# First turns of a feed-forward stage regrouped, attention scores over 128 rows, mLSTM gate rows by transfer

## The chip, the cores and the metric
The kernel runs on one core of a Trainium2 chip. Its time is the device time of one launch in microseconds (us). Matmuls run on TensorE (PE in the rows), elementwise work on VectorE (DVE), activations and copies on ScalarE (ACT), and small work on GpSimd (POOL). SyncE (SP) issues the weight transfers, GpSimd the others.

## The reference, cut to what matters
Two blocks of two layers each, on 256 tokens (two tiles of 128) and width 1024. Twelve stages run one after the other: in each layer a feed-forward stage, a mixer and a feed-forward stage. All eight feed-forward stages have an inner width of 2816.

```python
def swiglu_2(h, w_in, w_out):
    g, u = jnp.split(h @ w_in, 2, axis=-1)
    return (jax.nn.silu(g) * u) @ w_out
```

Block one ends each stage with a LayerNorm over the residual. Block two scales by an RMS norm ahead of and behind each stage. The mixer of block two has eight attention heads of width 64, whose scores of query and key are masked and weighted over all 256 tokens, and four mLSTM heads of width 128 in two directions. For head h and direction d the kernel computes, over all pairs of tokens s and t at once and with a as the key's gate value and m the running maximum,

```
w[s, t] = exp(a[s] - m[t])  where s <= t (d = 0) or s >= t (d = 1), else 0
num[t]  = sum_s w[s, t] * (k[s] . q[t]) * [v[s], 1]
cell[t] = sum over both directions of num[t] / max(|its last column|, exp(m)-term)
```

The cells are normed per head, gated, joined to the attention's output and multiplied with the output weights.

## The kernel before
**Numbers.** Every matmul with weights is done in three passes, high part by high part, high by low and low by high, of float32r operands. ScalarE copies a weight unit (128x1024) from its staging buffer to its high part `w_hi` (L286), VectorE subtracts to get the remainder `w_lo` (L293). There are 4 staging buffers and a ring of 10 units. SyncE loads unit u once the remainder of unit u - 4 is made. All engines walk through their lists of instructions in an order that is written out by hand and wait for each other by semaphores; there is no planner. `hi_upto` and `lo_upto` say up to which unit the weights are to be split at this point of the list.

**Feed-forward stage** (`pe_ffn`, `act_ffn`, `dve_ffn`). The inner width goes in 11 steps of 256 columns, 0 to 10. A step has four units of gate-and-up weights and two of down weights. In the unit order v = 0 to 65, the down units of step i come behind the gate-and-up units of step i + 1. Tile 1 of the tokens runs six units behind tile 0 (in stage 0 both run together for the first ten units). A tile of `hidden`, which is silu(gate) times up for 128 tokens and 256 columns, written (tile, step), must be turned before its down products: by TensorE (two transposes, L444) or by VectorE (`dve_turn_blocks`, 16 transposes of 32 rows, L468, for one tile or for two tiles at once). Then ScalarE takes the high part (L546) and VectorE the remainder `mt_lo` (L550), and TensorE waits for the latter. `pe_turns` (L429) lists which tiles TensorE turns: (0,0), (0,10) and (1,10), in stage 0 also (1,0). `block_turns` (L447) gives VectorE's groups: the unit at which a group begins, its length in units, and its tiles. In the later stages (0,1) and (1,0) are one group that begins at unit 9 and lasts four units, in stage 0 (0,1) and (1,1) are one from unit 8 on. Behind that, (0,i+1) and (1,i) go together. The last one, (1,9), goes by itself from unit 62 to 64.

**Mixer of block two** (`pe_mix2`, `act_mix2`, `dve_mix2`, `pool_mix2`). TensorE makes queries and keys, turns them, and ScalarE copies the turned ones to `aqk_t` (L1594), two heads over each other in 128 rows. Then 32 slots follow, of convolution inputs and then of values and output gates; a head of attention is scored (`a_scores`, L1438, over its own 64 rows), turned (L1448) and multiplied with the values (L1459) between them. The last head is scored in slot 22. VectorE makes the mLSTM's gate rows by scans at the first head. Then for each mLSTM head `m_pair` does four score matmuls (two of two passes, L1512) and four (two of two passes, L1515) that spread the negated maxima of both directions over 128 rows; `args` on VectorE adds the key's column and the mask (L1860), ScalarE takes the exponential (L1685), `weights` multiplies with the scores (L1871), and `m_out` (L1533) forms the sums. Output units (`out_unit`) stand between the heads. `cells`, `forward`, `cells_sum`, `squares`, `cell_var` and `gated_cells` make the normed and gated cell, `turn_cells` (L1541) turns it: heads one and two together, then three, then four. GpSimd loads rows, sets margins and takes reciprocal roots.

## Time and profile before

| what | value |
|---|---|
| median of 3 runs | 2150.64 us (2150.47 to 2152.52) |
| profiled execution, its time | 2148.35 us |
| its span, first to last instruction | 2146.6 us |
| mean granted TensorE clock | 0.997 |
| TensorE busy | 2112.1 us, 98% of the span |
| VectorE, ScalarE, GpSimd busy | 1685.6, 1077.0 and 65.6 us (79%, 50%, 3%) |
| DMA | 393.70 MB, mean 183 GB/s |

A line of a view names engine, kernel line, operation and tiles as out<-in, with the shape and a count. Matmuls are pipelined: a matmul of 512 columns is shown 0.39 us long, while the next one starts 0.227 us after it. So costs on TensorE are read from start to start. A float32 matmul is two instructions in the trace. "Idle before" is the time in which the engine had nothing to do, and the name behind it is what ended it. The granted clock is 1.00 at 2.4 GHz and 0.50 at 1.2 GHz.

### The profile page before, as it was taken

Reading aid. Unit: us, or ns where it says so; the run is one execution under the profiler, and the core shown is the slowest. Engines: PE = TensorE matmul, PEld = TensorE weight load, DVE = VectorE, ACT = ScalarE, POOL = GpSimd, SP = SyncE. Lnnn points to the kernel's source line nnn. Section 1 sums busy time; section 2 is a strip of 40 time slices with the busy share of each in tenths; the row PEclk is TensorE's granted clock in tenths of the full one; section 3 lists DMA queues with packets and bytes.
Section 4 is the critical chain, followed back from the end, with each engine's and each line's share of the span. In section 5 each row is a group of like instructions: output and inputs, shape, how many; then the busy total and the mean of one; then the engine's idle time right before and its main releaser. Section 6 shows DMA issues by size and latency. Waiting matters only on the chain.

```text
span 2146.6 us, 28816 instructions
## 1 busy us (share of the span) xinstructions
PE 2112.1 (98%) x10580; PEld 1778.2 (83%) x10580; DVE 1685.6 (79%) x3108; ACT 1077.0 (50%) x1540; POOL 65.6 (3%) x107
## 2 busy tenths in 40 slices
PE   8999999999999999999999999999999999999998
PEld 6888999888788899988877888877887888888887
DVE  6888766888888867678888886788887888678886
ACT  5444553544544455454454446564445445665443
POOL 0000010000000001000000000010000000001000
PEclk9999999999999999999999999999999999999999
DMA  7766754666666574666656656337666665644663
GB/s 232 236 198 179 214 177 148 208 195 196 196 192 194 167 233 141 193 196 196 191 185 195 195 178 189 111 119 224 189 193 188 186 194 160 186 132 140 195 190 105
DMA packets 313951, 393.70 MB, mean 183 GB/s; under 512 B 17828, under 2 KB 272052, under 8 KB 313812
## 3 DMA queue, kind: packets, MB, share of 16 engines
q1 hardware_dynamic: 309120, 375.52, 57.6%
q0 software_dynamic: 4528, 16.29, 2.4%
q8 instruction: 84, 1.38, 0.2%
q14 instruction: 55, 0.45, 0.1%
q10 hardware_dynamic: 164, 0.06, 0.0%
HBM read 390.75 MB, written 1.05 MB: 183 GB/s over the span
## 4 chain that ended last, share of the span: by engine, by line
PE 84%; DVE 9%; DMA 3%; issue 2%; ACT 2%; SPq 0%; POOL 0%; DVEq 0%; POOLq 0%; ACTq 0%
PE bank L309 23%; PE bank L311 23%; PE bank L310 23%; DVE w_lo L293 5%; PE bank L303 3%; PE bank L304 3%; PE bank L305 3%; DVE hidden L468 2%; DMA stage<-in_ffn_w_in 1%; DMA stage<-in_w_in 1%; DMA stage<-in_ffn_w 1%; PE bank L1438 1%; ACT w_hi L286 1%; PE bank L1459 1%; PE bank L482 1%
## 5 line engine op out<-in xcount | busy, mean ns | idle before, releaser
L286 ACT ACTIVATE w_hi<-stage 128x1024 fp32r<-128x1024 f32 x711 | 746.2, 1058 | 681.8 <-PE bank L311 534.0
L293 DVE TENSOR_TENSOR w_lo<-stage,w_hi 128x1024 fp32r<-128x1024 f32 x711 | 865.4, 1224 | 259.1 <-ACT w_hi L286 252.6
L309 PE MATMUL bank<-w_hi,xt_hi 128*128 128x512 f32 x1760 | 691.8, 393 | 0.6 <-DVE w_lo L293 0.2
L311 PE MATMUL bank<-w_hi,xt_lo 128*128 128x512 f32 x1760 | 685.8, 390 | 0.0
L310 PE MATMUL bank<-w_lo,xt_hi 128*128 128x512 f32 x1760 | 685.6, 390 | 0.0
L468 DVE STREAM_TRANSPOSE hidden<-hidden 32x128 f32<-32x128 f32 (+1 forms) x1280 | 377.6, 295 | 21.0
L309 PEld LDWEIGHTS bank<-w_hi,xt_hi 128*128 128x128 f32 x1760 | 330.9, 188 | 71.7 <-issue 3.1
L311 PEld LDWEIGHTS bank<-w_hi,xt_lo 128*128 128x128 f32 x1760 | 330.6, 188 | 69.6
L310 PEld LDWEIGHTS bank<-w_lo,xt_hi 128*128 128x128 f32 x1760 | 331.0, 188 | 66.3
L309 PE MATMUL bank<-w_hi,mt_hi 128*128 128x512 f32 x768 | 305.6, 398 | 20.0 <-DVE mt_lo L550 20.0
L311 PE MATMUL bank<-w_hi,mt_lo 128*128 128x512 f32 x768 | 301.2, 392 | 0.0
L310 PE MATMUL bank<-w_lo,mt_hi 128*128 128x512 f32 x768 | 300.6, 391 | 0.0
L309 PEld LDWEIGHTS bank<-w_hi,mt_hi 128*128 128x128 f32 x768 | 145.1, 189 | 56.0 <-DVE w_lo L293 22.9
L311 PEld LDWEIGHTS bank<-w_hi,mt_lo 128*128 128x128 f32 x768 | 145.0, 189 | 31.0
L310 PEld LDWEIGHTS bank<-w_lo,mt_hi 128*128 128x128 f32 x768 | 145.3, 189 | 28.2
L303 PE MATMUL bank<-xt_hi,w_hi 128*128 128x256 f32 x512 | 148.9, 291 | 0.0
L305 PE MATMUL bank<-xt_hi,w_lo 128*128 128x256 f32 x512 | 144.8, 283 | 0.0
L304 PE MATMUL bank<-xt_lo,w_hi 128*128 128x256 f32 x512 | 144.8, 283 | 0.0
L303 PEld LDWEIGHTS bank<-xt_hi,w_hi 128*128 128x128 f32 x512 | 98.0, 191 | 4.0 <-issue 3.8
L304 PEld LDWEIGHTS bank<-xt_lo,w_hi 128*128 128x128 f32 x512 | 98.0, 192 | 0.7 <-issue 0.5
L305 PEld LDWEIGHTS bank<-xt_hi,w_lo 128*128 128x128 f32 x512 | 98.0, 191 | 0.0
L546 ACT ACTIVATE mt_hi<-hidden 128x256 fp32r<-128x256 f32 x151 | 54.3, 404 | 35.9 <-DVE hidden L468 35.9
(266 smaller groups left out, 1381.4 us busy)
## 6 DMA issues: line engine op xcount, KB each, us to landing
stage<-in_ffn_w SPq DMA_DIRECT2D x352, 256.0 KB, 3.2
stage<-in_ffn_w_in SPq DMA_DIRECT2D x352, 256.0 KB, 3.2
stage<-in_ffn_w SPq DMA_DIRECT2D x88, 512.0 KB, 3.7
stage<-in_ffn_w_out SPq DMA_DIRECT2D x88, 512.0 KB, 3.7
stage<-in_w_in SPq DMA_DIRECT2D x80, 512.0 KB, 4.3
stage<-in_mix_w_in SPq DMA_DIRECT2D x56, 512.0 KB, 4.3
stage<-in_w_out SPq DMA_DIRECT2D x16, 512.0 KB, 4.2
stage<-in_mix_w_out SPq DMA_DIRECT2D x16, 512.0 KB, 3.5
```

The source lines that it names most:

```text
L286: act.activation(w_hi[:, u % RING, :], stage[:, u % STAGED, :], ACT.Copy).then_inc(S["hi_ready"], 1)
L293: dve.tensor_tensor(w_lo[:, u % RING, :], stage[:, u % STAGED, :], f32(w_hi[:, u % RING, :]), ALU.subtract).then_inc(S["lo_ready"], 1)
L303: pe.matmul(o, hi, m_hi, start=first, stop=False)
L304: pe.matmul(o, hi, m_lo, start=False, stop=False)
L305: return pe.matmul(o, lo, m_hi, start=False, stop=last)
L309: pe.matmul(o, m_hi, hi, start=first, stop=False)
L310: pe.matmul(o, m_hi, lo, start=False, stop=False)
L311: return pe.matmul(o, m_lo, hi, start=False, stop=last)
L468: ins = dve.transpose(h_t[32 * b:32 * b + 32, c, p], h32_blocks[p, c, b, :])
L482: mm = pe.transpose(acc[:, t, k * P:(k + 1) * P], src[:, t, k * P:(k + 1) * P], ident)
L546: act.activation(ht_hi[:, t, i % 2], turned_h(s, t, i), ACT.Copy).then_inc(S[f"h_hi{t}"], 1)
L1438: mm = pe.matmul(bank[:, 0, i * T:(i + 1) * T], aqk_t[p0:p0 + 64, h // 2, i * P:(i + 1) * P], aqk_t[p0:p0 + 64, 4 + h // 2, :], start=True ...
```

## The change
- TensorE turns (0,0) and (1,0) in all feed-forward stages, in stage 0 also (0,1) and (1,1). VectorE's groups begin with (0,1) alone, turned in unit 7, its high part at 9 (in stage 0 with (0,2), turned in units 16 and 17). The pairs behind stand as before, and (1,9) is turned in units 63 and 64, its high part at 65. The high part and the remainder of (0,10) are taken ahead of that unit's weight split and not behind it.
- The attention scores run over 128 rows: even heads read the upper half of `aqk_t` with zeros in the query below it, odd heads a query of their own with zeros above it. GpSimd writes the zeros.
- GpSimd writes the negated maxima of both directions to DRAM and reads them back with one transfer of 8 x 256 float32 into each of 128 partitions. It masks the diagonal blocks by four selections. ScalarE takes the exponential with the key's column as its bias, four per head; `m_pair` without its broadcasts is `m_scores`, which has two banks in turn. `args` and the two tables of masks go.
- The denominators of both directions are made in one instruction each. Weight splitting in the mLSTM is ordered anew, and so are cells and output units; head one is turned alone, heads two and three in a row.

```diff
         def pe_turns(s):
 
-            return ([(1, 0)] if s == 0 else []) + [(0, 0), (0, STEPS - 1), (1, STEPS - 1)]
+            return [(0, 0), (1, 0)] + ([(0, 1), (1, 1)] if s == 0 else []) + [(0, STEPS - 1), (1, STEPS - 1)]
 
         def turned_count(s, t, i):
-            before = ffn_no(s) * 3 + (1 if s else 0)
-            order = [(0, 0)] + [e for e in pe_turns(s) if e != (0, 0)]
-            return before + order.index((t, i)) + 1
+
+            return ffn_no(s) * 4 + (2 if s else 0) + pe_turns(s).index((t, i)) + 1
...
         def block_turns(s):
 
-            begin = {}
-            for v in range(UNITS["ffn"]):
-                for i in range(STEPS):
-                    for t, u in ((0, v), (1, behind(s, v))):
-                        if u == gu_end(i) and (t, i) not in pe_turns(s):
-                            begin.setdefault(9 if s and t + i == 1 else v + 1, []).append((t, i))
-            return [(v, 2 * len(tiles), sorted(tiles)) for v, tiles in sorted(begin.items())]
+
+            first = [(7, 1, 9, [(0, 1)])] if s else [(16, 2, 18, [(0, 2)])]
+            both = [(6 * i + 8, 4, 6 * i + 12, [(0, i + 1), (1, i)]) for i in range(1 if s else 2, STEPS - 2)]
+            return first + both + [(63, 2, 65, [(1, STEPS - 2)])]
...
+                if v == turn_after(STEPS - 1) + 1:
+                    act_h(act, s, 0, STEPS - 1)
                 hi_upto(act, b + v + RING - LAG)
                 if s == 0 and v == TOGETHER + 3:
                     act_lower_bounds(act)
-                for g, (v0, length, tiles) in enumerate(block_turns(s)):
-                    if v == v0 + length:
+                for g, (_, _, v1, tiles) in enumerate(block_turns(s)):
+                    if v == v1:
                         for t, i in tiles:
                             act_h(act, s, t, i, g)
                 for i in range(STEPS):
...
+                if v == turn_after(STEPS - 1) + 1:
+                    dve_h(dve, s, 0, STEPS - 1)
                 lo_upto(dve, b + v + RING - LAG)
                 if s == 0 and v == TOGETHER + 2:
                     dve_tables(dve)
                 if s == 0 and v == TOGETHER + 4:
                     dve_lower_bounds(dve)
-                for v0, length, tiles in block_turns(s):
-                    if v == v0 + length:
+                for _, _, v1, tiles in block_turns(s):
+                    if v == v1:
                         for t, i in tiles:
                             dve_h(dve, s, t, i)
                 for i in range(STEPS):
...
-                p0 = 64 * (h % 2)
+                q = (q_odd if h % 2 else q_even)[h // 2]
                 for i in range(NT):
-                    mm = pe.matmul(bank[:, 0, i * T:(i + 1) * T], aqk_t[p0:p0 + 64, h // 2, i * P:(i + 1) * P],
-                                   aqk_t[p0:p0 + 64, 4 + h // 2, :], start=True, stop=True)
+                    mm = pe.matmul(bank[:, 0, i * T:(i + 1) * T], q[:, i * P:(i + 1) * P], aqk_t[:, 4 + h // 2, :],
+                                   start=True, stop=True)
...
-            def m_pair(h):
+            def m_scores(h):
 
                 if h == 0:
                     pe.wait_ge(S["mo_out"], at("mo_out", L, 2))
                     pe.wait_ge(S["conv_silu"], at("conv_silu", L))
-                else:
-                    pe_hold(pe, S["m_p"], at("m_p", L, 4 * h))
+                if h >= 2:
+                    pe.wait_ge(S["m_p"], at("m_p", L, 4 * (h - 1)))
                 for j in range(NT):
-                    pe.matmul(m_s[:, j, :], conv_y[:, 4 + h, j * P:(j + 1) * P], conv_y[:, h, :],
-                              start=True, stop=True)
-                for d in range(2):
-                    mm = pe.matmul(m_bc[:, d, :], ident[0:8, d * H + h:d * H + h + 1].broadcast_to([8, P]),
-                                   g_neg_rows[d], start=True, stop=True)
+                    mm = pe.matmul(m_s2[:, h % 2, j, :], conv_y[:, 4 + h, j * P:(j + 1) * P], conv_y[:, h, :],
+                                   start=True, stop=True)
                 mm.then_inc(S["m_scores"], 1)
...
             def turn_cells(h):
+
+                pe.wait_ge(S["m_out"], at("m_out", L, 2 * h + 2))
+                pe.wait_ge(S["m_p"], at("m_p", L, 12 if h < 2 else 16))
+                if h % 2:
+                    pe.wait_ge(S["m_lo"], at("m_lo", L, 2 + h))
                 for i in range(NT):
                     mm = pe.transpose(merged[:, h, i * P:(i + 1) * P], cell[:, i, h * P:(h + 1) * P], ident)
-                return mm
-
-            m_pair(0)
+                mm.then_inc(S["mg_turned"], 1)
+
+            def late_unit(h):
+
+                pe.wait_ge(S["m_lo"], at("m_lo", L, 3 + h))
+                return out_unit(0, 4 + h)
+
+            m_scores(0)
+            m_scores(1)
             pe.wait_ge(S["m_lo"], at("m_lo", L, 2))
-            for t in range(NT):
-                out_unit(t, 0)
-            for h in range(1, H):
-                m_pair(h)
-                m_out(h - 1)
-                out_unit(0, h)
+            out_unit(0, 0)
+            m_out(0)
+            m_scores(2)
+            out_unit(1, 0)
+            m_out(1)
+            m_scores(3)
+            out_unit(0, 1)
+            m_out(2)
             out_unit(1, 1)
-            pe.wait_ge(S["m_p"], at("m_p", L))
-            pe.wait_ge(S["m_out"], at("m_out", L, 4))
             turn_cells(0)
-            turn_cells(1).then_inc(S["mg_turned"], 1)
-            m_out(H - 1)
-            out_unit(1, 2)
-            pe.wait_ge(S["m_out"], at("m_out", L, 6))
-            turn_cells(2).then_inc(S["mg_turned"], 1)
-            pe.wait_ge(S["m_lo"], at("m_lo", L, 3))
-            out_unit(0, 4)
-            out_unit(0, 5)
-            pe.wait_ge(S["m_out"], at("m_out", L))
-            turn_cells(3).then_inc(S["mg_turned"], 1)
-            pe.wait_ge(S["m_lo"], at("m_lo", L, 4))
-            out_unit(0, 6)
-            pe.wait_ge(S["m_lo"], at("m_lo", L))
-            out_unit(0, 7).then_inc(S["acc_done0"], 1)
-            for k in range(3, KD):
+            out_unit(0, 2)
+            m_out(3)
+            out_unit(0, 3)
+            turn_cells(1)
+            turn_cells(2)
+            late_unit(0)
+            late_unit(1)
+            turn_cells(3)
+            late_unit(2)
+            late_unit(3).then_inc(S["acc_done0"], 1)
+            for k in range(2, KD):
...
-                for n in range(2):
-                    act.activation(aqk_t[:, 4 * n:4 * n + 4, t * P:(t + 1) * P],
-                                   bank[:, 4 + 2 * t + n, :].rearrange("p (k n) -> p k n", k=4), ACT.Copy)\
-                       .then_inc(S["a_t_out"], 1)
+                act.wait_ge(S["rot"], at("rot", L))
+                src = bank[:, 4 + 2 * t, :].rearrange("p (k n) -> p k n", k=4)
+                c = slice(t * P, (t + 1) * P)
+                act.activation(aqk_t[0:64, 0:4, c], src[0:64], ACT.Copy).then_inc(S["a_t_out"], 1)
+                for n, part_ in enumerate(q_odd_parts):
+                    act.activation(part_[64:P].rearrange("p (k n) -> p k n", k=2)[:, :, c], src[64:P, 2 * n:2 * n + 2],
+                                   ACT.Copy).then_inc(S["a_t_out"], 1)
+                act.activation(aqk_t[:, 4:8, c], bank[:, 5 + 2 * t, :].rearrange("p (k n) -> p k n", k=4), ACT.Copy)\
+                   .then_inc(S["a_t_out"], 1)
 
...
+            def exps(h):
+
+                if h == 0:
+                    act.wait_ge(S["m_masked"], at("m_masked", L))
+                    act.wait_ge(S["g_cols"], at("g_cols", L))
+                if h >= 2:
+                    act.wait_ge(S["m_num"], at("m_num", L, 2 * h - 2))
+                for d in range(2):
+                    for j in range(NT):
+                        c0, c1, p0 = m_cols(d, j)
+                        row = m_bc[:, d, h, :] if c1 - c0 == T else m_diag[:, d, h, :]
+                        act.activation(m_w[:, h % 2, d, p0:p0 + c1 - c0], row, ACT.Exp,
+                                       bias=g_cols[:, 0, d, j, d * H + h:d * H + h + 1]).then_inc(S["m_exp"], 1)
+
+            hi_upto(act, b + 34)
+            exps(0)
...
+            def merged_hi(h):
+                act.wait_ge(S["mg_turned"], at("mg_turned", L, 2 + h))
+                act.activation(mt_hi[:, 4 + h, :], merged[:, h, :], ACT.Copy).then_inc(S["m_hi"], 1)
+
+            for d in range(2):
+                act.activation(g_em[:, d], g_cols[:, 1, d, :, d * H:(d + 1) * H], ACT.Exp).then_inc(S["g_em"], 1)
+            exps(1)
+            hi_upto(act, b + 35)
+            forward(0)
+            exps(2)
+            squares(0)
+            forward(1)
+            exps(3)
+            squares(1)
+            forward(2)
+            merged_hi(0)
+            squares(2)
+            hi_upto(act, b + 36)
+            forward(3)
+            merged_hi(1)
+            squares(3)
+            merged_hi(2)
+            hi_upto(act, b + 37)
+            merged_hi(3)
             hi_upto(act, b + 40)
...
+            weights(1)
             dve.wait_ge(S["g_em"], at("g_em", L))
-            dve.tensor_scalar(g_em, g_em, float(P) ** 0.5, None, ALU.mult).then_inc(S["k_scaled"], 1)
-            dve.wait_ge(S["k_scaled"], at("k_scaled", L))
-            lo_upto(dve, base + 37)
-            for h in range(1, H):
-                args(h)
-                if h >= 2:
-                    cell_var(h - 2)
-                weights(h)
-                cells(h - 1)
-                if h >= 2:
-                    gated_cells(h - 2)
-                cells_sum(h - 1)
-                if h == 1:
-                    lo_upto(dve, base + 38)
-
-            def merged_rest(n, k):
-                dve.wait_ge(S["m_hi"], at("m_hi", L, n))
-                dve.tensor_tensor(mt_lo[:, k, :], merged[:, k.start - 4:k.stop - 4, :], f32(mt_hi[:, k, :]),
-                                  ALU.subtract).then_inc(S["m_lo"], 1)
-
-            cell_var(H - 2)
-            merged_rest(3, slice(4, 6))
-            cells(H - 1)
-            gated_cells(H - 2)
-            cells_sum(H - 1)
-            cell_var(H - 1)
-            merged_rest(4, slice(6, 7))
-            gated_cells(H - 1)
-            lo_upto(dve, base + 39)
-            merged_rest(5, slice(7, 8))
-            lo_upto(dve, base + 40)
+            cells(0)
+            cells_sum(0)
+            weights(2)
+            cells(1)
+            cell_var(0)
+            cells_sum(1)
+            gated_cells(0)
+            weights(3)
+            cells(2)
+            cell_var(1)
+            cells_sum(2)
+            merged_rest(0)
+            gated_cells(1)
+            cell_var(2)
+            lo_upto(dve, base + 35)
+            cells(3)
+            gated_cells(2)
+            cells_sum(3)
+            merged_rest(1)
+            cell_var(3)
+            merged_rest(2)
+            gated_cells(3)
+            lo_upto(dve, base + 36)
+            merged_rest(3)
+            lo_upto(dve, base + 38)
...
+            pool.wait_ge(S["margins"], at("margins", L, 3))
+            pool.memset(q_odd_parts[1][0:64], 0.0).then_inc(S["margins"], 1)
+            pool.wait_ge(S["margins"], at("margins", L, 4))
+            pool.wait_ge(S["x_turned"], xt_at(s, 1, 1))
+            pool.memset(aqk_t[64:P, 0:4, :], 0.0).then_inc(S["margins"], 1)
+            pool.wait_ge(S["margins"], at("margins", L, 5))
+            pool.wait_ge(S["rot"], at("rot", L))
+            pool.memset(q_odd_parts[0][0:64], 0.0).then_inc(S["margins"], 1)
+            pool.wait_ge(S["g_scan"], at("g_scan", L, 8))
+            for d in range(2):
+                pool.dma_start(neg_dram[d * H:(d + 1) * H, :], g_neg_rows[d][d * H:(d + 1) * H, :])\
+                    .then_inc(S["neg_out"], 16)
+            pool.wait_ge(S["neg_out"], at("neg_out", L))
+            pool.wait_ge(S["a_scores"], at("a_scores", L))
+            pool.dma_start(m_bc.rearrange("p d h t -> p (d h t)"),
+                           neg_dram.rearrange("r t -> (r t)").partition_broadcast(P)).then_inc(S["bc_in"], 16)
+            pool_hold(pool, S["bc_in"], at("bc_in", L))
+            pool_hold(pool, S["xp_out"], at("xp_out", L))
+
+
+            for d, i, o in ((0, 0, m_bc[:, 0, :, 0:P]), (0, 1, m_diag[:, 0]), (1, 0, m_diag[:, 1]), (1, 1, m_bc[:, 1, :, P:T])):
+                sign = -1 if d else 1
+                pool.affine_select(o, m_bc[:, d, :, i * P:(i + 1) * P], [[0, H], [sign, P]], ALU.is_ge, -1e30, base=0,
+                                   channel_multiplier=-sign).then_inc(S["m_masked"], 1)
```

## Rows read from the trace of the kernel before

**Rows 1.** The page's first part, busy us (share of the span) x instructions

```profile
PE 2112.1 (98%) x10580; PEld 1778.2 (83%) x10580; DVE 1685.6 (79%) x3108; ACT 1077.0 (50%) x1540; POOL 65.6 (3%) x107
```

**Rows 2.** Whom TensorE waited for, us in total, times, longest us

```profile
PE bank L309 <- DVE mt_lo L550: 20.0, 15, 3.2
...
PE bank L1512 <- DVE scratch L1871: 0.5, 2, 0.2
```

**Rows 3.** TensorE's timeline at waits: start us, us, what [idle before <-releaser]

```profile
46.88 0.47 PE L309 MATMUL bank<-w_hi,mt_hi 128*128 128x512 f32 x1 [2.52 <-DVE mt_lo L550]
...
183.11 0.47 PE L309 MATMUL bank<-w_hi,mt_hi 128*128 128x512 f32 x1 [0.82 <-DVE mt_lo L550]
...
1653.28 0.39 PE L311 MATMUL bank<-w_hi,xt_lo 128*128 128x512 f32 x1
1656.87 0.76 PE L309 MATMUL bank<-w_hi,mt_hi 128*128 128x512 f32 x1 [3.20 <-DVE mt_lo L550]
...
1797.02 0.47 PE L309 MATMUL bank<-w_hi,mt_hi 128*128 128x512 f32 x1 [0.98 <-DVE mt_lo L550]
```

**Rows 4.** By windows: us, engines busy, granted clock, DMA share, GB/s

```profile
48.60:51.00 2.40, 2.40 (x7) 1.88 (x6) 1.16 (x2) 2.39 (x4) 0.00 (x0) 0.50 0.75 217
...
1657.50:1662.10 4.60, 4.60 (x12) 3.55 (x11) 2.59 (x6) 0.06 (x1) 0.00 (x0) 0.50 0.71 225
```

**Rows 5.** TensorE's timeline around one turn of a hidden tile

```profile
1602.97 0.38 PE L444 MATMUL bank<-const,hidden 128*128 128x128 f32 x2
...
1603.42 0.40 PE L310 MATMUL bank<-w_lo,mt_hi 128*128 128x512 f32 x1
```

**Rows 6.** VectorE's timeline, at a pair's turn and at a last turn

```profile
1646.31 1.25 DVE L468 STREAM_TRANSPOSE hidden<-hidden 32x128 f32<-32x128 f32 x4
...
1603.41 1.98 DVE L468 STREAM_TRANSPOSE hidden<-hidden 32x64 f32<-32x64 f32 x8
1605.40 1.22 DVE L293 TENSOR_TENSOR w_lo<-stage,w_hi 128x1024 fp32r<-128x1024 f32 x1
1606.54 0.41 DVE L550 TENSOR_TENSOR mt_lo<-bank,mt_hi 128x256 fp32r<-128x256 f32 x1
```

**Rows 7.** Timelines of VectorE and TensorE at stage 0's last gate

```profile
191.97 0.42 DVE L533 TENSOR_TENSOR hidden<-hidden,bank 128x256 f32<-128x256 f32 x1 [0.69 <-ACT hidden L524]
...
192.72 0.38 PE L444 MATMUL bank<-const,hidden 128*128 128x128 f32 x2
```

**Rows 8.** TensorE's timeline at the last attention scores and at 128-row float32 matmuls

```profile
1380.32 0.60 PE L1448 MATMUL bank<-const,scratch 128*128 128x128 f32 x4
...
1382.24 0.40 PE L310 MATMUL bank<-w_lo,xt_hi 128*128 128x512 f32 x1
...
319.66 1.89 PE L1038 MATMUL bank<-r,hidden 128*128 128x256 f32 x8
...
321.51 0.28 PE L304 MATMUL bank<-xt_lo,w_hi 128*128 128x256 f32 x1
```

**Rows 9.** TensorE's timeline at the first mLSTM head

```profile
1398.28 1.02 PE L1512 MATMUL bank<-r 128*128 128x256 f32 x4
1399.23 0.69 PE L1515 MATMUL bank<-hidden,const 8*128 8x256 f32 x2
...
1400.62 0.39 PE L310 MATMUL bank<-w_lo,mt_hi 128*128 128x512 f32 x1
```

**Rows 10.** GpSimd's timeline at selections, and landing times of a row transfer (L836)

```profile
296.20 2.15 POOL L1317 TENSOR_SCALAR_AFFINE_SELECT hidden<-hidden 128x128 f32<-128x128 f32 x4 [3.11 <-ACT hidden L1107]
...
DMA to landing us min/median/max: 5.4/6.5/7.7
```

**Rows 11.** ScalarE's timeline, and its group of exponentials (x count | busy, mean ns)

```profile
1388.28 1.28 ACT L1646 ACT_TABLE_LOAD   x1
...
1395.50 0.68 ACT L1655 ACTIVATE scratch<-bank,small 128x512 f32<-128x512 f32 x1
...
L1685 ACT ACTIVATE scratch<-hidden 128x384 f32<-128x384 f32 x16 | 8.4, 526 | 9.5 <-DVE hidden L1860 8.5
```

142 lines of the change are left out of this document (55 added, 87 removed).

## The prediction

> **What bounds the kernel now.** The first part of the page says that TensorE is busy for 98% of the span [rows 1]. In the chain of waits it also holds nearly everything, so a change pays only if it takes instructions off TensorE or takes away a time in which TensorE waits. The view of who TensorE waited for shows how little of the second kind there is: 20.0 us in 15 waits for the remainder `mt_lo` of a turned hidden tile, 0.5 us in two waits in the mLSTM, and small ones [rows 2]. In the timeline of TensorE I looked up where the 15 stand. Each of the eight feed-forward stages has one early on, ahead of the down products of (tile 0, step 1) and (tile 1, step 0), and all but the last have a second one in front of the last step's down products of tile 0. Two of each are shown, with what they cost from start to start [rows 3]: 1653.28 to 1656.87 is 3.59 us where two matmuls normally start 0.227 us apart, so the wait of 3.20 costs 3.36, and each wait costs 0.16 more than its idle time. The seven second ones lie between 0.80 and 1.02 us. They make 6.2 us of idle time, so the eight first ones make 13.8.
>
> Two first waits have a tail. Behind the one of stage 0 and the one of stage 9 the granted clock is 0.50, the 1.2 GHz level, after TensorE had stood still for 2.5 and 3.2 us [rows 4]. 12 matmuls there fill 4.60 us where they would take 2.7. Over both stretches (2.9 and 5.6 us long) that is 3.0 to 4.2 us lost; I take 4.0.
>
> **First turns.** A hidden tile is turned on VectorE by 16 small transposes or on TensorE by two. The change sends (tile 1, step 0) to TensorE in the seven later stages, and (0,1) and (1,1) in stage 0: nine tiles. On TensorE a turn costs little: from the two transposes to the second matmul behind them 0.45 us instead of 0.227, so 0.22 each [rows 5], 2.0 us in all. On VectorE the shared pair of turns took four transposes of 0.31 us between two weight remainders of 1.22, four times over; the lone (0,1) takes 0.25 each [rows 6], all 16 stand now in unit 7 instead of in 9 to 12, ahead of the late weights rather than behind them. In stage 9, the worst, I moved the steps by these durations: (0,1) is ready about 7 us before TensorE comes to its down products at 1653.5, and (1,0), which TensorE turns behind unit 11 (about 1648.1), has its remainder near 1651.2, so 2.3 us early. What is late next is the pair (0,2) and (1,1), needed at unit 20: VectorE has about 14 us of work per six units (six remainders of 1.22, 16 transposes of 0.31, 1.7 for gates and `mt_lo`) against 72 x 0.227 = 16.3 us of TensorE, and is ready about 3 us early. So all eight go: 13.8 + 8 x 0.16 = 15.0, with the clock 19.0, less 2.0: 17.0 us. Bounds: 8 (half the waits come back because VectorE is behind for another reason) and 19.
>
> **Last turns.** The seven second waits are worth 6.2 + 7 x 0.16 = 7.3 us. They come from VectorE's order: 1.98 us of transposes, then a remainder of 1.22, then the `mt_lo` that TensorE waits for [rows 6]. Moved ahead of the remainder and of the turn of (1,9), it is ready 1.8 us before it is needed, so these waits go. But VectorE then waits once for ScalarE's high part, and again because ScalarE's next weight starts later, and so it comes to the norm of tile 0 about 0.7 us later. In the four stages with a LayerNorm the gate of the last step ends at 192.39 and TensorE turns it at 192.72 [rows 7]: only 0.3 us between them. ScalarE squares the residual first, so that gate moves with the norm, and TensorE gets there sooner by 1 us and waits. There I expect nothing, or -0.2 each. In the three RMS-norm stages the gate waited for TensorE, so some 0.85 of 1.14 stays: 2.5. Sum 1.7; bounds -1 and 7.3.
>
> **Attention scores.** Today each head's group of four 64-row matmuls, with four transposes ahead of it and one weight matmul behind it, takes 1380.32 to 1382.24, 1.92 us. Eight 128-row matmuls of 256 columns and the weight matmul behind them take 1.85 us, at most 0.23 each and 0.216 if the last one has its own 0.12 [rows 8]. With 0.11 for a transpose [rows 5] the group would be 0.44 + 0.87 + 0.23 = 1.54: the saving is 0.38 us, and most of it is what it costs to go into and out of the 64-row form. Sixteen groups: 6.1 us. Bounds 0 and 6.5. ScalarE makes four copies per tile for it instead of two, ahead of the first scores, in a stretch in which ScalarE has time; where that cover is gone it costs some 0.8 us per layer. GpSimd's three memsets are far ahead.
> The Trainium skill, "TensorE: Matmul & The Clock Gate", section "Why this matters for your kernels", has it that a lone matmul over 32 rows takes as long as one over 128. By that this part is worth nothing and the sum is 6.1 us less. That is a rival below. The rows speak against it only through the cost of changing the form.
>
> **Gate rows by transfer.** The eight pairs of broadcasts over 8 rows leave TensorE. A head's four score matmuls, four broadcasts and the weight matmul behind take 1398.28 to 1400.62, 2.34 us [rows 9]; without broadcasts 0.87 + 0.23 = 1.10. That saves 1.24 us per head, 9.9 for eight. The two small waits (0.5 + 2 x 0.16) go too: 10.7. VectorE loses 32 additions with mask and is free earlier in the cells.
> In return there is a chain that was not there. After the last scores (over at 1381.9) GpSimd issues a transfer of 1 MB, four selections of 128x512 make the masks, ScalarE does the four exponentials of head 0, and only then the values and output gates of tile 0, for which TensorE's first mLSTM scores wait. TensorE gets to them 16.4 us after the last attention scores [rows 9]. Transfer: the second of two 512 KB rows issued back to back lands after 5.4 to 7.7 us, with its neighbour's 0.5 thus 6 to 8.3 [rows 10]; I take 7.6, and 10.5 as the upper end. Selections: four of 128x128 took 2.15 us [rows 10], so four of four times the length take 2.2 to 8.6; I take 5. ScalarE: a table load of 1.28, which may be hidden; exponentials by the row of 128x384 at least 1.05 and with four calls 1.5; values and gate 0.6 + 0.68 [rows 11]. Together 7.6 + 5 + 1.3 + 1.5 + 1.3 = 16.7 against 16.4; with bounds 11.5 and 23.2. So 0.3 us of wait, and about another 1.2 because behind it ScalarE's high parts, the output gates of tile 1 and the second head's exponentials all come later than before, and `m_out(1)` waits for the cells of head 0. That is 1.5 per layer, 3.0 in all (0 to 16). Net 7.7.
> The skill's "SBUF — State Buffer", "Who interferes with whom", says a GpSimd instruction that reads SBUF and a VectorE one with two SBUF inputs shut each other out for the whole instruction. VectorE's weight remainders are of that kind, and up to four selections would each wait for one. This trace's 2.15 us for four cannot be split here. By that rule the mask rival below is the likelier case.
>
> **Order of the cells.** The out products are dealt out anew between the heads, and TensorE does none more. Between `m_out(h)` and `m_out(h+1)` it has 0.87 us of scores and an out unit of six matmuls, 1.36, and the chain of denominator, forward cell and sum must fit into these 2.2 us as it fits today. Turning cells one and two separately and three and four in a row is even work. This is -0.7 us for near misses (0 to -3).
>
> **Sum.** 17.0 + 1.7 + 6.1 + 7.7 - 0.7 = 31.8 us. The profiled execution took 2148.35 us, 1.75 outside its span of 2146.6, and becomes 2116.6. The median of the runs stands 2.3 us above it; what I take away does not depend on that, so 2150.64 - 31.8 = 2118.8.
>
> **Rivals.**
> - *The mask chain is too long* (chance 0.20): transfer and selections at their upper ends, 23.2 us per layer. TensorE then waits 7 us and loses its clock for a while: 8 per layer instead of 1.5, 2132. For it: ScalarE stands behind the mask with work that has nothing to do with it. Against: both upper ends at once.
> - *VectorE is late for another reason* (0.10): the first waits come back in half, since in stages 8 and 9 the weights of the units 10 and 11 themselves land late. 2150.6 - 31.8 + 9 = 2128.
> - *64 rows are not dearer* (0.07): the scores give nothing, 2125. Against: 1.92 us for a group that adds up to 1.54.
> - *The last turns pay in full and the mask is hidden* (0.10): 5.6 + 3.0 more, 2110.
> - *Slower than before* (0.03): the mask chain takes over 32 us a layer instead of 16.7, because GpSimd's transfer of one row to 128 partitions or its long selection is several times dearer than the short ones of the trace. From 32.6 us on (16.4 and half of the 34.8 that the rest is worth, less 1.2 of what follows) the layer waits eat the gain; at 36 each the time is 2157.
> - The forecast holds 0.50.
>
> The range that holds 8 in 10 is 2111 to 2132: the likeliest's own is 2114 to 2123, and it reaches down to the full gain and up to the mask case. This kernel's runs differ by about 0.1%, so 0.2%, 4.3 us, is what can be told from no change. Faster by more than that 0.96, within it 0.01, slower 0.03.
>
> **What would show it.** The line of `mt_lo` in TensorE's waits falls from 20.0 us to under 5, and what is left stands at the last steps of the LayerNorm stages, now before the turn of (1,10) or the next stage's first matmul. No stretch at clock 0.50 in stages 0 and 9. The score matmuls have 128 rows and start 0.22 us apart. The wait ahead of the first mLSTM scores tells the mask chain: under 2 us, and released by ScalarE. The forecast is wrong if that wait is over 4 us, if first waits of over 1 us remain, or if a boundary wait over 1.5 us shows up in several stages.

## The result, and the profile after

The changed kernel takes 2128.27 us (median of 4 runs, 2127.92 to 2128.41), and the kernel before took 2151.58 in the same comparison: ratio 0.9887, interval 0.987 to 0.9904. The forecast said 2118.8 us in a range from 2111 to 2132. So the direction and the range held, while about 9 us of the expected gain are missing. The profiled executions stand at 2148.35 and 2128.41 us, spans 2146.6 and 2126.7: 19.9 us against the forecast's 31.8.

The first part of the page after, against [rows 1]: TensorE is busy 13.9 us less, VectorE 23.2 less, and GpSimd 18.9 more.

```profile
PE 2098.2 (99%) x10566; PEld 1778.8 (84%) x10566; DVE 1662.4 (78%) x3046; ACT 1080.0 (51%) x1568; POOL 84.5 (4%) x127
```

Whom TensorE waited for, after (us in total, times, longest us), against [rows 2]. The 20.0 us of `mt_lo` are 0.9. The line to look at is the new first one: TensorE waits for the normed and scaled `xh`, in order to turn it for the next stage.

```profile
PE bank L478 <- DVE xh L801: 8.3, 3, 4.1
...
PE bank L443 <- DVE hidden L529: 1.9, 4, 0.5
PE bank L309 <- DVE w_lo L293: 1.6, 1, 1.6
PE bank L309 <- DVE scratch L1817: 1.0, 2, 0.5
PE bank L309 <- DVE mt_lo L546: 0.9, 4, 0.2
...
PE bank L1451 <- ACT scratch L1651: 0.6, 2, 0.3
```

TensorE's timeline after has two such waits, both at the end of an mLSTM stage. Behind them the matmuls start 0.43 us apart instead of 0.227.

```profile
1424.13 1.97 PE L478 MATMUL bank<-const,xh 128*128 128x128 f32 x8 [3.95 <-DVE xh L801]
...
1427.18 0.63 PE L309 MATMUL bank<-w_hi,mt_hi 128*128 128x512 f32 x1
1427.61 0.63 PE L310 MATMUL bank<-w_lo,mt_hi 128*128 128x512 f32 x1
...
1934.51 1.87 PE L478 MATMUL bank<-const,xh 128*128 128x128 f32 x8 [4.11 <-DVE xh L801]
```

The window view names the granted clock (the column ahead of the DMA share): half of full for most of the stretch, the 1.2 GHz level.

```profile
1424.00:1430.00 6.00, 5.87 (x19) 5.01 (x20) 5.67 (x9) 3.50 (x8) 0.56 (x1) 0.54 0.45 133
```

Why `xh` is late is read backwards from 1424.13. VectorE makes the second half of `r` only at 1419.47, after 5.06 us of idling for ScalarE's first square (L736):

```profile
1413.73 0.68 DVE L723 TENSOR_TENSOR r<-bank,rows 128x512 f32<-128x512 f32 x1
1419.47 0.69 DVE L723 TENSOR_TENSOR r<-bank,rows 128x512 f32<-128x512 f32 x1 [5.06 <-ACT xh L736]
```

ScalarE's timeline shows that square behind two high parts of weights, each of which waited for its transfer:

```profile
1414.89 1.06 ACT L286 ACTIVATE w_hi<-stage 128x1024 fp32r<-128x1024 f32 x1 [1.92 <-DMA stage<-in_ffn_w_in]
1417.80 1.06 ACT L286 ACTIVATE w_hi<-stage 128x1024 fp32r<-128x1024 f32 x1 [1.85 <-DMA stage<-in_ffn_w_in]
1418.77 0.58 ACT L736 ACTIVATE xh<-bank 128x512 f32<-128x512 f32 x1
```

Those two transfers were issued on SyncE's queue at 1411.24 and 1412.71, because each needs a staging slot that a low part on VectorE sets free. VectorE makes these low parts at 1409.99 and 1411.46, behind the cells of the last head:

```profile
1411.24 0.88 SPq L276 DMA_DIRECT2D stage<-in_ffn_w_in  x2
...
1412.71 0.88 SPq L276 DMA_DIRECT2D stage<-in_ffn_w_in  x2
```

```profile
1411.46 2.35 DVE L293 TENSOR_TENSOR w_lo<-stage,w_hi 128x1024 fp32r<-128x1024 f32 x2
```

The kernel before made the low parts of the same units in one go ahead of its first head, whose scores start at 1398.28, and so issued the same two loads at 1395.71 and 1396.85:

```profile
1393.33 3.49 DVE L293 TENSOR_TENSOR w_lo<-stage,w_hi 128x1024 fp32r<-128x1024 f32 x3
```

This is a theory so far; the first experiment tests its last step, ScalarE's order.

### The profile page after: what moved, and what is told of

Same layout as the page of the kernel before. It is cut to its first block, busy times and chain, and to the rows that moved or that the text cites. A ratio compares the mean times of both kernels' runs of the same rounds, so it can differ in the third digit from the quotient of the medians.

```text
span 2126.7 us, 28762 instructions
## 1 busy us (share of the span) xinstructions
PE 2098.2 (99%) x10566; PEld 1778.8 (84%) x10566; DVE 1662.4 (78%) x3046; ACT 1080.0 (51%) x1568; POOL 84.5 (4%) x127
## 4 chain that ended last, share of the span: by engine, by line
PE 87%; DVE 7%; ACT 2%; DMA 2%; issue 1%; POOL 0%; SPq 0%; DVEq 0%; POOLq 0%; ACTq 0%
PE bank L309 25%; PE bank L311 25%; PE bank L310 25%; PE bank L305 3%; PE bank L304 3%; PE bank L303 3%; DVE w_lo L293 3%; PE bank L478 1%; DVE hidden L464 1%; ACT w_hi L286 1%; PE bank L972 1%; DMA stage<-in_mix_w_in 1%; PE bank L1533 1%; ACT scratch L1651 0%; DMA stage<-in_ffn_w_in 0%
## 5 line engine op out<-in xcount | busy, mean ns | idle before, releaser
L464 DVE STREAM_TRANSPOSE hidden<-hidden 32x128 f32<-32x128 f32 (+1 forms) x1264 | 365.1, 289 | 19.9
L517 ACT ACTIVATE hidden<-bank,scale 128x256 f32<-128x256 f32 x88 | 37.8, 471 | 68.9 <-PE bank L311 68.9
```

The source lines that it names most:

```text
L464: ins = dve.transpose(h_t[32 * b:32 * b + 32, c, p], h32_blocks[p, c, b, :])
L517: act.activation(h32[:, t, :], gu_bank(t, i)[:, 0:FB], ACT.Silu, scale=scale2[:, t:t + 1])\
```

## Experiments

Line numbers are those of the changed kernel where nothing else is said. All kernels were timed beside the kernel before, at 2150.57 and 2150.53 us in the two comparisons.

**1. The squares ahead of the late weights.**

```
-            hi_upto(act, b + 40)
+            hi_upto(act, b + 39)
+            act_norm_sq(act, s, 0)
             hi_upto(act, b + 41)
-            act_norm_sq(act, s, 0)
```

> The changed kernel with one edit in ScalarE's order at the end of each mLSTM stage: the two squares of the norm of tile 0 stand ahead of the high parts of the two weight units whose transfers land last, where in the changed kernel they stand behind them. Theory A: the new wait of 3.95 and 4.11 us ahead of the turn of x into the next stage, with the half clock behind it (about 2.0 us each), has this cause: the low parts are made later now, so four loads are issued from 1405.7 to 1413.8, ScalarE sits 1.9 and 1.9 us before two high parts, and the squares start at 1418.8 though the accumulator is ready before 1413.7. Then the squares start at about 1413.5, the first half of the normed x is there at about 1419.1, ahead of TensorE's 1420.2, both waits go, and the time is 2128.3 - 8.1 - 4.1 = 2116 us. Theory B: VectorE's late low parts, and not ScalarE's order, hold the norm: then over half of each wait stays and the time is 2122 to 2128 us. Theory C: the rows of the norm's gain arrive late, the time stays at 2128.

Measured: 2118.25 us (4 runs, 2117.23 to 2120.54), ratio 0.9849 [0.9834, 0.9864]. Theory A holds, 2 us short of its 2116. ScalarE's timeline has the squares at 1416.00 and 1417.01, and TensorE turns `xh` without idle time and at the full clock:

```profile
1416.00 0.60 ACT L736 ACTIVATE xh<-bank 128x512 f32<-128x512 f32 x1 [0.48 <-PE bank L311]
```

```profile
1422.61 1.03 PE L478 MATMUL bank<-const,xh 128*128 128x128 f32 x8
1423.40 0.48 PE L309 MATMUL bank<-w_hi,mt_hi 128*128 128x512 f32 x1
```

Measured from turn to turn of `x` of tile 1, the stretches around the two boundaries together are 12.1 us shorter than in the changed kernel: 8.1 of idle time, and about 4.0 that go with the half clock. The spans moved by 9.3 and the medians by 10.0, because this profile has 2.8 us elsewhere that the changed kernel's has not. 1.8 are in stage 5, where a wait drew the half clock (experiment 5), and 1.0 in stage 0, where a turned tile came late:

```profile
60.24 0.47 PE L309 MATMUL bank<-w_hi,mt_hi 128*128 128x512 f32 x1 [1.10 <-DVE mt_lo L546]
```

The wait in stage 0 comes and goes from run to run: none in the changed kernel's profile, 0.21, 0.41 and 0.89 us in those of experiments 2, 3 and 4. That the low parts' new place on VectorE is what makes the transfers late is read from the two traces alone; no run put them back.

**2. The feed-forward turns alone,** on the kernel before: `pe_turns`, `turned_count`, `block_turns` and the calls of `act_h` and `dve_h` of the changed kernel, nothing of the mixers.

> The kernel before with only the feed-forward turns of the changed one (first and last turns); both mixers as before. Theory A: the terms of the forecast for the first and last turns are right (17.0 and 1.7 us), and the changed kernel shows less in those stages only because two of them begin with the half clock left by the new boundary waits: 18.7 us less than before, 2132.9 us of 2151.6. Theory B: the turns themselves gained only what these stages show in the changed kernel, 14.6 us: 2137.0 us.

Measured: 2131.31 us (2129.9 to 2132.57), 19.3 us less than before, ratio 0.9908 [0.9893, 0.9923]. Theory A by the medians: the forecast's two terms were 18.7, and the 14.6 of Theory B lie outside the interval. By the two profiled spans (2146.6 and 2129.9) it is 16.7; the profiled execution of the kernel before is one of its faster ones.

**3. Scores over 64 rows again.**

```
                 q = (q_odd if h % 2 else q_even)[h // 2]
+                p0 = 64 * (h % 2)
...
-                    mm = pe.matmul(bank[:, 0, i * T:(i + 1) * T], q[:, i * P:(i + 1) * P], aqk_t[:, 4 + h // 2, :],
-                                   start=True, stop=True)
+                    mm = pe.matmul(bank[:, 0, i * T:(i + 1) * T], q[p0:p0 + 64, i * P:(i + 1) * P],
+                                   aqk_t[p0:p0 + 64, 4 + h // 2, :], start=True, stop=True)
```

> The changed kernel with its attention scores over 64 rows again (the upper or lower half of the same tiles), everything else as it is. The forecast's price: 0.38 us in each of 16 groups, 6.1 us, and the trace of the changed kernel shows a further 0.09 us at the turns ahead of 14 groups. Theory A: the scores' gain was mostly swallowed by new waits of TensorE for VectorE and ScalarE in the same stretch (1.0 of L309, 0.6 of L1451, and smaller ones; the stretch from the first scores to the mLSTM scores went from 64.8 to 63.4 us, not 61.7), so giving the 0.38 us back fills those waits: 2.7 to 4 us slower than the changed kernel, 2131 to 2132.3 us. Theory B: the waits have another cause (the copies now in four parts, the memsets), they stay, and it is 6 to 7.4 us slower, 2134.4 to 2135.7 us. Theory C: 64 rows cost nothing, 2128.3 us.

Measured: 2131.02 us (2130.23 to 2131.6), 2.8 us above the changed kernel. Theory A: the waits L1817 and L1451, 1.6 us together, are gone from TensorE's waits, which now go on like this:

```profile
PE bank L443 <- DVE hidden L529: 1.9, 4, 0.5
PE bank L309 <- DVE w_lo L293: 1.4, 1, 1.4
PE bank L309 <- DVE mt_lo L546: 1.3, 5, 0.4
PE bank L309 <- DVE xt_lo L816: 0.4, 2, 0.2
```

**4. The mask selections three times.**

```
-                pool.affine_select(o, m_bc[:, d, :, i * P:(i + 1) * P], [[0, H], [sign, P]], ALU.is_ge, -1e30, base=0,
-                                   channel_multiplier=-sign).then_inc(S["m_masked"], 1)
+                for _ in range(3):
+                    if done:
+                        pool.wait_ge(S["m_masked"], at("m_masked", L, done))
+                    done += 1
+                    pool.affine_select(o, m_bc[:, d, :, i * P:(i + 1) * P], [[0, H], [sign, P]], ALU.is_ge, -1e30,
+                                       base=0, channel_multiplier=-sign).then_inc(S["m_masked"], 1)
```

> The changed kernel with each of the four selections that lay the causal masks over the gate rows made three times, each behind the one before, which gives the same values. It makes the selections about as long (4 x 3 x 0.72 = 8.6 us and the waits between) as the forecast put them (4 x 2.15 us); in the changed kernel they took 2.8 us and ended 2.65 us ahead of the first exponential. Theory A: the mask chain has 2.65 us of slack on ScalarE and 0.6 us more ahead of TensorE's first output matmuls, and TensorE waits for what is over: 5.8 - 3.2 = 2.6 us and some half clock in each layer, 2128.3 + 5 to 7 = 2133.5 to 2135.5 us. Theory B: the chain is hidden whatever it takes, within 0.5 us of 2128.3.

Measured: 2145.07 us (6 runs, 2140.76 to 2146.39), 16.8 us above the changed kernel. Theory B is out, and Theory A has the place right and the size far too small. GpSimd's selections fill 10.05 us of its timeline, not 8.6, and ScalarE's first exponential waits 5.93 us for them. Behind the exponentials stand the values and gates that TensorE's first scores need (L1682), so TensorE waits 5.08 us in the first layer, not 2.6:

```profile
1393.27 0.51 ACT L1673 ACTIVATE scratch<-xh,small 128x256 f32<-128x256 f32 x1 [5.93 <-POOL xh L2004]
```

```profile
1395.95 1.65 PE L1515 MATMUL bank<-r 128*128 128x256 f32 x3 [5.08 <-ACT scratch L1682]
```

and then runs at half clock:

```profile
1395.90:1401.50 5.60, 5.55 (x14) 4.41 (x15) 4.71 (x12) 4.64 (x12) 0.54 (x1) 0.56 0.00 0
```

A layer's mixer grew by 7.8 and 7.9 us. The selections grew by 7.2 us, and the transfer ahead of them took 0.9 longer (1375.14 to 1383.18, against 1374.14 to 1381.32). TensorE saw 5.1 of these 8, so the chain has about 2.9 us of slack before it costs anything, near the 3.2 that the expectation put down. What comes on top of the waits is 2.8 and 3.2 us. The 5.6 us at a clock of 0.56 account for about 2.5 of it by my estimate; no run takes the two apart.

**5. The second turn in two pieces,** on experiment 1.

```
-            first = [(7, 1, 9, [(0, 1)])] if s else [(16, 2, 18, [(0, 2)])]
+            first = [(7, 2, 9, [(0, 1)])] if s else [(16, 2, 18, [(0, 2)])]
```

> The changed kernel with the squares first (2118.3 us) and one more edit in the feed-forward stages after the first: the sixteen block transposes of VectorE for the second turn of tile 0 are spread over two weight units (eight and eight) instead of one, so that a low part of weights stands between them. Theory A: the wait of 1.6 to 1.8 us for w_lo at 939.5 us, in the stage behind the second scan mixer, which the kernel before did not have, comes from these sixteen (4.0 us in one piece) standing ahead of a low part that is ready to be made; then it goes with the half clock behind it (eight intervals of 0.2 us longer), and the time is 2118.3 - 1.8 - 1.6 = 2115 us. Theory B: the second half comes too late for the turned tile in all eleven feed-forward stages that begin so, a wait for mt_lo of 0.3 us or more comes in each, and the time is 2118 us or more.

Measured: 2116.47 us (5 runs, 2114.78 to 2119.75), ratio 0.9841 [0.9828, 0.9855]. The `w_lo` wait is gone from TensorE's waits, so Theory A has the mechanism. VectorE's timeline in experiment 1 (first fence) and here (second) shows it:

```profile
935.08 3.98 DVE L464 STREAM_TRANSPOSE hidden<-hidden 32x64 f32<-32x64 f32 x16
939.09 2.36 DVE L293 TENSOR_TENSOR w_lo<-stage,w_hi 128x1024 fp32r<-128x1024 f32 x2
```

```profile
934.93 1.23 DVE L293 TENSOR_TENSOR w_lo<-stage,w_hi 128x1024 fp32r<-128x1024 f32 x1
936.19 1.99 DVE L464 STREAM_TRANSPOSE hidden<-hidden 32x64 f32<-32x64 f32 x8
938.21 1.23 DVE L293 TENSOR_TENSOR w_lo<-stage,w_hi 128x1024 fp32r<-128x1024 f32 x1
```

Its profiled span is 3.7 us shorter than in experiment 1 (2113.7 and 2117.4), 3.1 of it in this stage. The medians differ by 1.8 with intervals that overlap, so that it is faster than experiment 1 is likely and not shown by the times. A wait of 0.86 us for a gate (L526) has come in the next feed-forward stage, which is 1.1 us longer than in experiment 1. This may be a small part of Theory B.

**6. The last gate earlier in the LayerNorm stages,** on experiment 5.

```
+            if s < BLOCK2:
+                act_silu(act, s, 1, STEPS - 1)
+                act_norm_sq(act, s, 0)
...
+                dve_norm_start(dve, s, 0, lambda: dve_gate(dve, s, 1, STEPS - 1))
+                dve_norm_var(dve, s, 0)
+                dve_h(dve, s, 1, STEPS - 1)
+                dve_norm_x(dve, s, 0)
```

The gate is made ahead of the second long operation in `dve_norm_start`.

> The kernel of the run before this one (squares first, first turns split) and, in the feed-forward stages of the first block alone, the last gate and turn of tile 1 ahead of the norm's work of tile 0: ScalarE makes the silu before the square, VectorE the gate between the two long operations of the norm, and the low part of the turned tile before the normed x. Theory A: the waits of 0.47 us for the gate and of 0.22 us for mt_lo, in four stages (0.63 and 0.39 us over the usual interval), which the forecast left standing, are of this order: 4 x 1.0 us less than the run before it, about 2111 us. Theory B: the normed x of tile 0 becomes late instead (it is about 0.9 us later, and the turn has 1.0 us), and the time stays or grows by up to 2 us.

Measured: 2116.79 us (2114.75 to 2120.31): no gain, Theory B. The four gate waits are gone and others stand in their place (line numbers are 12 higher here). 2.8 us of waits were taken away in the four stages (1.9 for the gate, 0.9 for `mt_lo`), and about 3.5 came. Only 0.7 of them are for the normed `x` that Theory B named; the rest are for the low part of the turned `x` behind it. The wait L526 of experiment 5 is gone as well:

```profile
PE bank L309 <- DVE xt_lo L828: 3.1, 5, 0.9
...
PE bank L478 <- DVE xh L813: 1.0, 2, 0.7
```

**7. The last turns as before.** The edits of the last turns undone in the changed kernel:

```
-        return first + both + [(63, 2, 65, [(1, STEPS - 2)])]
+        return first + both + [(62, 2, 64, [(1, STEPS - 2)])]
...
-                if v == turn_after(STEPS - 1) + 1:
-                    act_h(act, s, 0, STEPS - 1)
...
-                    if v == turn_after(i) + 1 and i < STEPS - 1 and (0, i) in pe_turns(s):
+                    if v == turn_after(i) + 1 and (0, i) in pe_turns(s):
```

and the same for VectorE.

> The changed kernel with only the last turns of the feed-forward stages as before (the last group one unit earlier, and the last turned tile of token tile 0 behind the weight units). It prices the forecast's second term, 1.7 us with bounds of -1 and 7.3. Theory A: the term holds: 2128.3 + 1.7 = 2130.0 us, all of it in the last three feed-forward stages of the second block. Theory B: the last turns bring nothing, 2128.3 us, and the 19.3 us of the turns alone are the first turns'. Theory C: they bring most of their upper bound, 2133 us or more.

Measured: 2132.24 us (2129.85 to 2134.17), 4.0 above the changed kernel by the medians, and 2.9 by the spans (2129.6 and 2126.7). TensorE's waits have a line again that the changed kernel holds at 0.9:

```profile
PE bank L309 <- DVE mt_lo L546: 6.2, 7, 1.0
```

From turn to turn of `x` of tile 1 it is 1.24, 1.22 and 1.27 us in the three RMS-norm stages, 3.7 together, and within 0.3 of nothing in those with a LayerNorm. Between Theory A (1.7) and Theory C (5), with A's place.

**8. The mixers alone,** experiment 1 with the feed-forward code of the kernel before.

> Both mixer changes (scores over 128 rows; gate rows by transfer and the new order) with the squares first, but the feed-forward turns of the kernel before. Theory A: the parts add, the turns' 19.3 us come on top of 2118.3: 2137.5 us, 13 us less than before. Theory B: the turns and the mixers share a gain or a loss at their boundaries (clock, late weights): then it is 2134 us or less, or 2140 or more.

Measured: 2139.55 us (2136.82 to 2139.81), 11 us less than before, 2 less than if the parts added up (32.3 - 19.3 = 13.0). The interval of the ratio, 0.993 to 0.9957, reaches 2.9 us to either side, so the times alone do not tell A from B. The profile says where the difference is: the old first waits are there again, and vary.

```profile
PE bank L309 <- DVE mt_lo L550: 21.9, 15, 3.9
```

In stage 6, which no mixer change touches, the first wait is 3.86 us here and was 2.77 before, and the stage is 3.9 us longer from turn to turn of `x` (1101.08 to 1292.37, against 1101.30 to 1288.73). The clock behind the wait is 0.50 here (1139.8 to 1144) and was 1.00. Stages 8 and 9 moved as well, by 3.2 and -1.7 us. The two mixer stages are 6.9 and 7.2 us shorter than before, 14.0 together. So the shortfall lies outside the mixers, and such a stage has no fixed price. Whether regrouped turns take this spread away is not shown: the four runs of the changed kernel lie within 0.5 us, the five of experiment 5 within 5.0.

## Why the prediction was right, and where it was not

Direction and range held, but the measured time is outside the 2114 to 2123 of the forecast's likeliest case. It equals the 2128 of a rival, *VectorE is late for another reason*, by coincidence: that rival wanted half of the first waits back, and the changed kernel has none of them. The steps one by one:

**First turns (17.0 forecast).** The mechanism was right and the size somewhat high. The eight waits and both half-clock stretches are gone (granted clock 1.00 over 45 to 52 us and over 1640 to 1665). By experiments 2 and 7 the first turns bring 19.3 less 4.0, 15.3 us, by the medians, and 16.7 less 2.9, 13.8 us, by the spans. Most of the difference is in stage 5, behind the second scan mixer, where the weights land late and the sixteen transposes in unit 7, which the forecast put "ahead of the late weights", stand in front of a low part instead. That wait of 1.60 us is in the trace after, and experiment 5 took it away:

```profile
939.55 0.50 PE L309 MATMUL bank<-w_hi,xt_hi 128*128 128x512 f32 x1 [1.60 <-DVE w_lo L293]
```

From turn to turn of `x` of tile 1 that stage is 0.6 us longer than before in the changed kernel and 2.4 longer in experiment 2, where the forecast counted on 1.4 less. It had worked out stage 9 as the worst stage, and stage 5 was another case.

**Last turns (1.7).** The split was right: nothing with a LayerNorm, where the trace has the wait that it announced, and a gain in the three RMS-norm stages.

```profile
189.43 0.44 PE L443 MATMUL bank<-const,hidden 128*128 128x128 f32 x2 [0.47 <-DVE hidden L529]
```

The size was low: experiment 7 has 1.24 us in each of the three and not 0.85, so 3.7 and not 1.7, and 2.9 (spans) to 4.0 us (medians) over the whole kernel.

**Attention scores (6.1).** The group's price was exact in its sum. Four transposes, four score matmuls and the weight matmul behind them take 1372.12 to 1373.66, 1.54 us, where [rows 8] had 1.92:

```profile
1372.12 0.60 PE L1451 MATMUL bank<-const,scratch 128*128 128x128 f32 x4
1372.55 1.03 PE L1441 MATMUL bank<-xh,scratch 128*128 128x256 f32 x4
1373.23 0.59 PE L309 MATMUL bank<-w_hi,xt_hi 128*128 128x512 f32 x1
1373.66 0.40 PE L310 MATMUL bank<-w_lo,xt_hi 128*128 128x512 f32 x1
```

The step that failed was the next one: the forecast took all sixteen savings as time won. From the first attention scores to the first mLSTM scores the stretch is 64.77 us before (1333.51 to 1398.28) and 63.44 after (1326.28 to 1389.72), 1.33 and not 3.05 a layer, and experiment 3 prices the whole at 2.8 us. TensorE reached the products sooner than VectorE and ScalarE had the logits and exponentials ready: the waits L1817 and L1451 are 0.8 us a layer, and of the seven stretches from one head's turn (L1451) to the next, 6.7 to 6.9 us long before, four are 0.3 to 0.4 us shorter and three, with 6.97, 6.84 and 7.13 us, are not. In this timeline of VectorE two low parts stand ahead of the sum that TensorE waits for:

```profile
1359.01 2.36 DVE L293 TENSOR_TENSOR w_lo<-stage,w_hi 128x1024 fp32r<-128x1024 f32 x2 [1.16 <-ACT w_hi L286]
1361.29 0.69 DVE L1817 TENSOR_TENSOR scratch<-bank,hidden 128x512 f32<-128x512 f32 x1
```

The rival that 64 rows are not dearer is out by the time of the group, but not because a matmul over 64 rows is slower. In the middle of the group two instructions take the same time over 64 rows (first fence, before) and over 128 (second, after), 0.21 us from start to start:

```profile
1381.16 0.59 PE L1438 MATMUL bank<-xh 64*128 64x256 f32 x2
```

```profile
1372.77 0.59 PE L1441 MATMUL bank<-xh,scratch 128*128 128x256 f32 x2
```

The 0.38 us stand at the ends of the group: 0.10 at the transposes ahead (0.53 and 0.43), 0.10 behind the first score matmul (0.32 and 0.22), and 0.19 from the last one to the second weight matmul (0.65 and 0.46). So this trace agrees with the sentence of the Trainium skill that was weighed there ("TensorE: Matmul & The Clock Gate", "Why this matters for your kernels"), as far as 64 rows show it. What failed is what the rival drew from it, that the part is worth nothing: it left out the cost of changing the form, which the forecast had named as most of its 0.38.

**Gate rows by transfer, and the order of the cells (7.7 and -0.7).** Better than forecast on TensorE. From the first mLSTM scores to the turn of `x` it was 36.10 us (1398.28 to 1434.38); after it is 34.41 (1389.72 to 1424.13) with 3.95 of wait in it, so 30.46 without. That is 5.64 a layer, 5.62 in the second: 11.3 us. Experiment 1, which has no such wait, bears it out: its mixer stage is 138.74 us from turn to turn of `x` against 145.65, and the 6.9 are 5.6 and the 1.3 of the scores. The gross term of 10.7 held, and neither the 3.0 for the mask chain nor the 0.7 for near misses came. No run takes the transfer and the new order apart, so the 11.3 belong to both. The mask chain in GpSimd's timeline:

```profile
1374.14 0.56 POOL L1991 DMA_DIRECT2D xh<-neg_rows  x1 [36.16 <-PE bank L1441]
1381.32 0.84 POOL L1999 TENSOR_SCALAR_AFFINE_SELECT xh<-xh 128x512 f32<-128x512 f32 x1 [6.62 <-DMA xh<-neg_rows]
1382.13 1.40 POOL L1999 TENSOR_SCALAR_AFFINE_SELECT hidden<-xh 128x512 f32<-128x512 f32 x2
1383.48 0.63 POOL L1999 TENSOR_SCALAR_AFFINE_SELECT xh<-xh 128x512 f32<-128x512 f32 x1
```

```profile
1386.76 0.51 ACT L1673 ACTIVATE scratch<-xh,small 128x256 f32<-128x256 f32 x1
```

The transfer takes 7.0 us to landing (forecast 7.6), the four selections 2.8 (forecast 5, bounds 2.2 to 8.6). They end 2.65 us before ScalarE, which stands at a table load, wants them. Experiment 4 shows that the rival was no idle one: with the selections at 10 us a layer loses 7.8, the 8 that the rival had put down. (The forecast's lower bound of 11.5 for the chain does not follow from its own lowest terms, 6 + 2.2 + 1.05 + 1.3 = 10.6; nothing rests on it.)

The forecast also weighed whether a GpSimd instruction that reads SBUF and a VectorE one with two SBUF inputs wait for each other. The traces show them longer where they meet. In experiment 4 a selection that started inside a weight remainder took 1.49 us, where most take 0.63:

```profile
1386.30 1.49 POOL L2004 TENSOR_SCALAR_AFFINE_SELECT hidden<-xh 128x512 f32<-128x512 f32 x1
```

```profile
1386.07 1.22 DVE L293 TENSOR_TENSOR w_lo<-stage,w_hi 128x1024 fp32r<-128x1024 f32 x1 [0.21 <-ACT w_hi L286]
```

In the second layer the same pair took 1.43 and 1.65 us. In the changed kernel the selections met one VectorE instruction of this kind (L1828 at 1381.58, 0.86 us where the median is 0.48), and the chain was still in time.

**What was missed.** The other step that failed, and the one that cost the most, is "Order of the cells". It followed TensorE alone ("TensorE does none more") and costed the work behind the cells at nothing. But the same edit moved four low parts on VectorE, three from ahead of the first head and one from between the heads, to the last head and behind it (1404.50 to 1413.8). Each frees a staging slot, so SyncE's loads for the next stage moved too; ScalarE's high parts waited for these, and the squares of the norm stood behind the high parts in ScalarE's order. Two waits of 3.95 and 4.11 us and about 4 us of half clock: 12.1 us, next to the 11.9 by which the spans fell short of the forecast. With experiment 1 the same change is at 2118.25 us, and the forecast was 2118.8. This agreement is in part luck, since scores gave 3.3 less, the first turns 1.7 to 3.2 less, the last turns about 2 and the mLSTM 4.3 more than their terms, and by the spans experiment 1 gains 29.2 and not 31.8. That the changed kernel still fell into the range is luck too: the range was drawn for other reasons. The last sentence of the forecast had named "a boundary wait over 1.5 us" in several stages as what would prove it wrong; it stands in two.

Both kernels are beaten by experiments 1, 5 and 6, at 2116.5 to 2118.3 us, and I would keep experiment 5: 34 us less than before.

## What to carry to other kernels

Where an order is written by hand, list for each instruction that you move what it releases, up to the load queue, and what stands behind those loads on every other engine; an edit that makes one engine's work late can stop a third one that has nothing to do with it. In an in-order engine put what is on the path ahead of what waits for a transfer. And a saving on the bounding engine counts only up to the lead that its suppliers have in that stretch: read the lead before adding the saving up.

## What the runs showed of the hardware

- A selection over 128x512 on GpSimd took 0.63 us where it met no VectorE instruction with two inputs from SBUF, and one over 128x128 took 0.54 [rows 10]: four times the elements for 1.2 times the time. Those that met one took 0.81 to 0.94 us in the changed kernel and up to 1.49 in experiment 4.
- Two transfers of a weight unit issued 1.47 us apart reached ScalarE 3.65 and 5.1 us after issue (1411.24 to 1414.89, 1412.71 to 1417.80).
- A wait of 1.60 us in stage 5 had no half clock behind it in the changed kernel (granted clock 1.00 over 939.5 to 944.5), and one of 1.80 us at the same place in experiment 1 had (0.64 over 940.3 to 945.0). It makes such a wait cost 1.8 or about 3.5 us, and is one reason why sums of parts miss by 2 us here.

```profile
939.50:944.50 5.00, 4.95 (x23) 4.07 (x24) 4.07 (x5) 1.36 (x2) 0.00 (x0) 1.00 0.70 226
```

```profile
940.30:945.00 4.70, 4.63 (x15) 3.61 (x15) 4.09 (x6) 1.37 (x2) 0.00 (x0) 0.64 0.62 191
```
